# Experts of a routed mixture: a block's down product stands between the two halves of the next block's gate and up products

## The chip, the cores and the metric

The kernel runs on one core of one Trainium2 chip. The metric is the device time of one execution in microseconds. The kernel before takes 1736.07 us, the median of 3 runs (1735.58 to 1736.92).

In the text PE is TensorE, DVE is VectorE, ACT is ScalarE, POOL is GpSimd and SP is SyncE, as the profile writes them.

## The reference

One layer of a backbone over 1024 latent tokens and 256 context tokens of width 1024: modulation, one input projection into two groups of heads (a gated delta rule and a differential attention), an output projection, a layer norm, and then a mixture of experts, which is the part that the change touches. Each token chooses 2 of 32 experts, and an expert is a SwiGLU of width 512:

```
def block_ffn(args):
    xb, e = args
    return (jax.nn.silu(xb @ w_gate[e]) * (xb @ w_up[e])) @ w_down[e]
```

So a block of tokens has three products with its expert's weights: gate and up (1024 to 512 each), and then down (512 to 1024), which needs the result of the first two. All is float32. The outputs of a token's two experts are weighted and added in the last stage.

## The kernel before

The kernel is a row of stages, each of which ends with a barrier of all engines. The stage of the change is `experts`. Its work is a list of blocks of 32 token rows, sorted by expert; how many blocks there are, and which expert each has, is computed on the chip by the stage before. Four blocks are a quad (128 rows): the tokens of a quad are gathered from memory together, turned by PE (L2717, `turn_x`, at the start of each quad's body, for the next quad) and stored together by ACT (L2797).

What happens to one block b, by engine:

- PE makes the gate and up products in one go, `hidden(b, ...)` (L2725), eight steps of the contraction in two halves of four; each half waits until the weights of its last step are in `now["hidden"]`. The down product is `down(b, ...)` (L2737), four steps. It waits for the turned hidden rows of its block (`h_turned`) and for all four parts of `now["down"]` (`copied["down"]`).
- ACT takes the silu of the gate half (`gate`, L2775), after the last step of `hidden(b)`.
- DVE multiplies by the up half (L2835) and turns the result by 32x32 squares (L2839); both are `mix`. Later it scales the down product into the output tile (`keep_y`, L2831).

The weights of the current expert lie in one set of tiles, `now["hidden"]` and `now["down"]`, that PE reads. SP loads the next experts' weights from memory into `raw` tiles (L2336), three places deep for gate and up and two for down; a place is loaded again once its copy has been made. Where the expert changes between block b and block b+1, the new weights are copied over the old ones, part by part as PE has done with each:

- DVE copies the gate and up weights (`copy_hidden`, L2819, eight copies) while PE is at `hidden(b)`, ahead of `mix(b)` in DVE's program.
- ACT copies the down weights (`copy_down`, L2782, four copies) in its body for block b, each after PE has done the step of `down(b)` that reads the old ones.

All of it is written as one body for each block, and each engine runs its own body in order. ACT's body for block b is, in this order:

```
shape(i + u, 1 - u, X_PARTS[s])
gate(b + 1, (s + 1) % SUBS)
with act.If(here < after):
    copy_down(here + 1, b)
```

`shape` (L2767) writes a part of the next quad's turned tokens. `gate(b + 1)` waits for all eight steps of `hidden(b + 1)`, so the copies of `copy_down` stand behind it. PE's body works one block ahead in the same way: in the body of block b stand `hidden(b + 1)` and `down(b)`.

Of the kernel before, what the change touches and what calls it, by code (L numbers as in the profile page):

```python
# [2576 lines left out]
def experts(m):  # L2577
# [34 lines left out]
    def blocks(eng, start=None, block=None, end=None):  # L2612


        nb = eng.value_load(plan[0:1, PLAN_BLOCKS:], min_val=LOW * SUBS, max_val=BLOCKS)

        def run(part, *of):
            if part:
                part(*of)

        with ExitStack() as deeper:
            for q in range(QUADS):
                if q >= LOW:
                    deeper.enter_context(eng.If(nb > q * SUBS))
                run(start, q, q // 2, q % 2)
                with ExitStack() as inner:
                    for s in range(SUBS if block else 0):
                        if q >= LOW and s:
                            inner.enter_context(eng.If(nb > q * SUBS + s))
                        block(q, q // 2, q % 2, s)  # L2630
                run(end, q, q // 2, q % 2)
        return nb

    def place_of(eng, b):

        return eng.value_load(ranks[0:1, b:b + 1], min_val=0, max_val=NE - 1)
# [18 lines left out]
    def by_blocks(ap):  # L2655
        return ap.rearrange("p (w b x) -> p w b x", w=2, x=SUB)

    def columns_of(ap, j):

        return ap.rearrange("p w (b j x) -> p j w b x", j=SUBS, x=SUB)[:, j]  # L2660

    def hidden_bank(s):
        return m.bank(2 + s % 2, 2 * P)

    def down_bank(s):
        return m.bank(5 + s % 2, WIDE)

    with nc.Block() as block:
        @block.sync
        def _(sp):  # L2670
            experts_ = sp.value_load(plan[0:1, PLAN_EXPERTS:PLAN_EXPERTS + 1], min_val=2, max_val=NE)
            nq = sp.value_load(plan[0:1, PLAN_QUADS:PLAN_QUADS + 1], min_val=LOW, max_val=QUADS)
            def follow(place, u):

                for part in expert_loader(m, sp, place, u, copied if u > 1 else None):
                    part()

            AHEAD = 2 * SLOTS
            follow(1, 1)
            with sp.If(2 < experts_):  # L2680
                follow(2, 2)
            with sp.Fori(0, (NE - 3 + AHEAD - 1) // AHEAD) as i:
                for u in range(3, 3 + AHEAD):
                    with sp.If(AHEAD * i + u < experts_):
                        follow(AHEAD * i + u, u)

            sp.wait_ge(copied["hidden"], experts_ * KD)
            for t in range(TL):
                sp.dma_start(x1[t][:, :], d["x1"][t]).then_inc(early, 16)
            sp.dma_start(rep_ln[:, :, :], d["rep_ln"].rearrange("p (w n) -> p w n", w=4)[:, 2:4, :]).then_inc(early, 16)  # L2690

            sp.wait_ge(nothing_ready, 1)
            with sp.Fori(0, QUADS - LOW) as j:
                with sp.If(nq < j + LOW + 1):
                    sp.dma_start(flat(one(ybq, j + LOW)).rearrange("p (k n) -> p k n", k=KD), nothing[:, :].unsqueeze(1).to_broadcast([P, KD, D // KD])).then_inc(nothing_stored, 16)
                with sp.If(j + LOW < nq):
                    sp.sem_inc(nothing_stored, 16)
            sp.wait_ge(nothing_stored, 16 * (QUADS - LOW))
            sp.sem_inc(all_stored, 1)
# [11 lines left out]
        @block.tensor  # L2711
        def _(pe):
            def turn_x(i, u):
                pe.wait_ge(gathered[u], 16 * i + 16)
                pe.wait_ge(x_kept[1 - u], i + u)
                for k in range(KD):
                    last = nc.tensor.transpose(m.bank(k // 4)[:, k % 4 * P:(k % 4 + 1) * P], xg[u][:, k * P:(k + 1) * P], ident)  # L2717
                last.then_inc(x_turned[u], 1)

            def hidden(b, u, s, place, ks):  # L2720

                pe.wait_ge(copied["hidden"], place * KD + ks[-1] + 1)
                for k in ks:
                    for j in range(SUBS):
                        last = nc.tensor.matmul(by_blocks(hidden_bank(s)[j * SUB:(j + 1) * SUB, :]), xm[u][:, k, s * SUB:(s + 1) * SUB],  # L2725
                                                columns_of(now["hidden"][:, :, k, :], j), start=(k == 0), stop=(k == KD - 1),
                                                tile_position=(0, j * SUB))
                    last.then_inc(used["hidden"], 1)

            def down(b, s, place):  # L2730
                pe.wait_ge(h_turned, b + 1)
                if b >= 1:
                    pe.wait_ge(y_kept, b - 1)
                pe.wait_ge(copied["down"], place * KE + KE)
                for k in range(KE):
                    for j in range(SUBS):
                        last = nc.tensor.matmul(down_bank(s)[j * SUB:(j + 1) * SUB, :], hT[s % 2][:, k * SUB:(k + 1) * SUB],  # L2737
                                                now["down"][:, k, j * WIDE:(j + 1) * WIDE], start=(k == 0), stop=(k == KE - 1),
                                                tile_position=(0, j * SUB))
                    last.then_inc(used["down"], 1)  # L2740

            def body(q, i, u, s):
                b = q * SUBS + s
                here, after = place_of(pe, b), place_of(pe, b + 1)
                v, r = (u, s + 1) if s + 1 < SUBS else (1 - u, 0)
                if r == 0:
                    pe.wait_ge(x_kept[v], i + u + 1)
                pe.wait_ge(mixed, b)
                hidden(b + 1, v, r, after, range(KD // 2))
                hidden(b + 1, v, r, after, range(KD // 2, KD))  # L2750
                down(b, s, here)

            turn_x(0, 0)
            pe.wait_ge(x_kept[0], 1)
            first = place_of(pe, 0)
            hidden(0, 0, 0, first, range(KD // 2))
            hidden(0, 0, 0, first, range(KD // 2, KD))
            blocks(pe, lambda q, i, u: turn_x(i + u, 1 - u), body)

        @block.scalar  # L2760
# [310 lines left out]
```

## Time and profile before

| | |
|---|---|
| median of 3 runs | 1736.07 us |
| the profiled execution | 1734.94 us |
| its span | 1733.1 us |
| PE busy | 1517.3 us, 88% of the span |
| DVE busy | 927.7 us, 54% |
| ACT busy | 692.2 us, 40% |
| first `hidden` in a block's body | 1204.73 us |
| last `down` | starts at 1667.91 us |
| gate and up matmuls (L2725) | 4992, of 293.7 us in all |
| down matmuls (L2737) | 2464, of 147.4 us in all |
| blocks with a down product | 77 |
| changes of expert | 21 |

One execution was profiled, and its times run from the start of the span. Every matmul of the program stands twice in the trace: one block has 32 for gate and up in the program and 64 rows in the trace, and 16 and 32 for down. The 77 blocks follow from 2464 rows by 32, the 21 changes from the 84 copies of L2782 by four. Matmuls overlap, so busy time is not a sum of their durations. A row of the timeline gives the start, the time that it covers, engine, line, operation and tiles, and how many instructions it merges; in brackets stands the idle time of the engine ahead of it and what ended that.

### The profile page before, as it was taken

The numbers are of one execution on the slowest core, as the hardware profiler recorded it, in microseconds if no ns is written. First come the engines' busy times: TensorE is split into PE (matmuls) and PEld (weight loads), VectorE is DVE, ScalarE is ACT, GpSimd is POOL, SyncE is SP. The second block draws the span as 40 slices with busy tenths as digits, with TensorE's granted clock in tenths as the row PEclk, the third lists the DMA queues.
The fourth block names the chain that finished last, engine by engine and source line by source line (L and its number), as shares of the span: only waits on it lengthen the run. The fifth ranks groups of instructions, "written<-read, shape, count | busy, mean of one in ns | idle before, by whom it ended". The sixth has DMA issues, their size and how long they took to land. (4 is left out here: it accounts for less than half of the span.)

```text
span 1733.1 us, 47260 instructions
## 1 busy us (share of the span) xinstructions
PE 1517.3 (88%) x19436; PEld 1107.4 (64%) x19436; DVE 927.7 (54%) x1862; ACT 692.2 (40%) x1585; POOL 191.5 (11%) x266
## 2 busy tenths in 40 slices
PE   5799998999968899979998888954999999998768
PEld 3588885779857788856666567743555555554333
DVE  6798752341124565658999846774142454343416
ACT  5544431012234545536667734422141433433321
POOL 0000100000043544400000000000000000000015
PEclk9899998999978999989999998966999999999989
DMA  9312315450133344230020044318849789999976
GB/s 360 122 61 80 128 46 203 172 176 26 61 121 108 114 124 118 85 138 19 13 74 19 7 144 158 122 52 324 309 174 346 290 322 397 398 397 393 358 233 256
DMA packets 154396, 305.33 MB, mean 176 GB/s; under 512 B 10718, under 2 KB 57390, under 8 KB 150834
## 3 DMA queue, kind: packets, MB, share of 16 engines
q1 hardware_dynamic: 132306, 244.94, 39.1%
q0 software_dynamic: 10336, 46.67, 7.6%
q10 hardware_dynamic: 11520, 10.49, 1.9%
q8 instruction: 161, 2.64, 0.6%
q14 instruction: 73, 0.60, 0.1%
HBM read 256.40 MB, written 45.66 MB: 174 GB/s over the span
## 5 line engine op out<-in xcount | busy, mean ns | idle before, releaser
L2725 PE MATMUL psum<-now_hidden,i_xm 128*32 128x256 f32 x4992 | 293.7, 388 | 23.7 <-DVE now_hidden L2819 17.2
L2725 PEld LDWEIGHTS psum<-now_hidden,i_xm 128*32 128x32 f32 x4992 | 160.1, 112 | 149.4 <-issue 32.6
L2737 PE MATMUL psum<-now_down,i_hT 128*32 128x256 f32 x2464 | 147.4, 379 | 5.8 <-ACT now_down L2782 5.8
L2835 DVE TENSOR_TENSOR i_h<-i_silu,psum 128x128 f32<-128x128 f32 x78 | 22.3, 286 | 215.7 <-ACT i_silu L2775 215.7
L2767 ACT ACTIVATE i_xm<-psum,modT 128x128 f32<-128x128 f32 x163 | 63.3, 457 | 161.7 <-issue 130.0
L2819 DVE COPY now_hidden<-raw_hidden 128x1024 f32 x168 | 104.1, 694 | 36.5 <-DMA raw_hidden<-in_w_up 27.9
L2737 PEld LDWEIGHTS psum<-now_down,i_hT 128*32 128x32 f32 x2464 | 81.0, 110 | 59.2 <-ACT now_down L2782 9.1
L1911 PE MATMUL psum<-dkT,f_qT 64*128 64x512 f32 (+1 forms) x384 | 90.4, 577 | 23.7 <-ACT f_E L1962 21.2
L123 PE MATMUL psum<-hT_head,wm_head 128*128 128x512 f32 (+1 forms) x256 | 97.6, 381 | 10.7 <-DVE hT_rest L414 6.4
L1962 ACT ACTIVATE f_E<-psum,f_mx 128x1280 f32<-128x1280 f32 (+2 forms) x96 | 92.1, 967 | 15.8 <-DVE f_mx L2021 15.7
L123 PE MATMUL psum<-hT_head,wm_rest 128*128 128x512 f32 (+1 forms) x256 | 96.0, 375 | 0.0
L123 PE MATMUL psum<-hT_rest,wm_head 128*128 128x512 f32 (+1 forms) x256 | 95.7, 374 | 0.0
L2782 ACT ACTIVATE now_down<-raw_down 128x1024 f32 x84 | 81.9, 1054 | 12.9 <-DMA raw_down<-in_w_down 8.5
L2775 ACT ACTIVATE i_silu<-psum 128x128 f32<-128x128 f32 x78 | 21.7, 278 | 162.9 <-PE psum L2725 162.2
L1931 PE MATMUL psum<-dv,f_AT 128*128 128x128 f32 x640 | 85.3, 279 | 0.8 <-ACT f_AT L1968 0.6
L1931 PEld LDWEIGHTS psum<-dv,f_AT 128*128 128x128 f32 x640 | 78.4, 194 | 6.5 <-issue 3.0
L123 PE MATMUL psum<-wt_rest,hT_head 128*128 128x512 f32 x208 | 82.2, 395 | 0.0
L1968 ACT ACTIVATE f_AT<-psum 128x512 f32<-128x512 f32 (+1 forms) x96 | 50.5, 526 | 71.7 <-PE psum L1921 71.7
L1494 ACT ACTIVATE e_pc<-psum 128x128 f32<-128x128 f32 x100 | 26.5, 284 | 126.0 <-PE psum L1354 124.9
L661 DVE SCALAR_TENSOR_TENSOR conv<-padded,cw,conv 128x1282 f32<-128x1282 f32 x48 | 74.6, 1555 | 1.7
L2282 PE MATMUL psum<-w_out_head,g_yT 128*128 128x512 f32 x128 | 56.2, 439 | 14.8 <-ACT g_yT L1794 10.4
L2020 DVE TENSOR_REDUCE f_mx<-psum 128x1 f32<-128x768 f32 x64 | 60.8, 951 | 15.0 <-PE psum L1911 15.0
(377 smaller groups left out, 2986.5 us busy)
## 6 DMA issues: line engine op xcount, KB each, us to landing
raw_hidden<-in_w_gate SPq DMA_DIRECT2D x22, 2048.0 KB, 19.9
raw_hidden<-in_w_up SPq DMA_DIRECT2D x22, 2048.0 KB, 24.9
raw_down<-in_w_down SPq DMA_DIRECT2D x22, 2048.0 KB
wa_late<-in_w_ada POOLq DMA_DIRECT2D x16, 1024.0 KB, 5.5
yb<-i_y ACTq DMA_DIRECT2D x80, 128.0 KB, 7.4
wa<-in_w_ada SPq DMA_DIRECT2D x8, 1024.0 KB, 13.2
wt<-in_w_in SPq DMA_DIRECT2D x4, 2048.0 KB, 7.8
wm<-in_w_in SPq DMA_DIRECT2D x12, 512.0 KB, 3.7
```

The source lines that it names most:

```text
L123: last = nc.tensor.matmul(out, a, b, start=(first and n == 0), stop=(final and n == 2))
L661: ins = nc.vector.scalar_tensor_tensor(y, padded[u][:, j:j + wide], cw[:, c * CONV + j:c * CONV + j + 1], y, ALU.mult, ALU.add)
L1911: last = nc.tensor.matmul(scores(c, key, key + w), qT[t % 2][rows, h, :], dkT[rows, h, key:key + w], start=True, stop=True)
L1931: last = nc.tensor.matmul(m.bank(7, P, h * P), AT[n % 2][:, t, :], dv[:, t, h * P:(h + 1) * P], start=(t == 0), stop=(t == TT - 1))
L1962: nc.scalar.activation(E[n % 2][c][:, a:z], scores(c, a, z), ACT.Exp, bias=mx[n % 2][c][:, 2:3], scale=SC, accum_out=rs[n % 2][c][:, part: ...
L2020: link(nc.vector.tensor_reduce(x[:, 1:2], scores(c, NC, TOK), AX, ALU.max))
L2282: nc.tensor.matmul(m.bank(2 + c), yT[t % 2][:, k, :], w[:, k, here], start=(k == 0 and n == 0), stop=False)
L2725: last = nc.tensor.matmul(by_blocks(hidden_bank(s)[j * SUB:(j + 1) * SUB, :]), xm[u][:, k, s * SUB:(s + 1) * SUB], columns_of(now["hidden" ...
L2737: last = nc.tensor.matmul(down_bank(s)[j * SUB:(j + 1) * SUB, :], hT[s % 2][:, k * SUB:(k + 1) * SUB], now["down"][:, k, j * WIDE:(j + 1) ...
L2767: last = nc.scalar.activation(xm[u][:, k, :], m.bank(k // 4)[:, k % 4 * P:(k % 4 + 1) * P], ACT.Identity, scale=modT[:, 4 * KD + k, 0:1], ...
L2782: nc.scalar.activation(now["down"][:, k, :], down_slot(place, k), ACT.Copy).then_inc(copied["down"], 1)
L2819: nc.vector.tensor_copy(now["hidden"][:, :, k, :], loaded[:, :, k, :]).then_inc(copied["hidden"], 1)
```

## The change

In PE's body for a block, `down(b)` moves ahead of the second half of `hidden(b + 1)`. Nothing else changes: the same instructions, with the same waits, on every engine.

```diff
                 pe.wait_ge(mixed, b)
                 hidden(b + 1, v, r, after, range(KD // 2))
+                down(b, s, here)
                 hidden(b + 1, v, r, after, range(KD // 2, KD))
-                down(b, s, here)
```

On PE, the body of the first block and the start of the second stood in this order before (L2722 is the wait of a half of `hidden`, L2734 that of `down`, L2636 loads the blocks' places in the list of experts):

```order
L2636 TENSOR_LOAD ranks
L2636 ISA x2
L2722 ISA
L2725 MATMUL psum<-now_hidden,i_xm_15268 32x256 x16
L2722 REGISTER_ALU
L2725 MATMUL psum<-now_hidden,i_xm_15268 32x256 x16
L2734 ISA
L2737 MATMUL psum<-now_down,i_hT_15265 32x256 x16
L2636 TENSOR_LOAD ranks
L2636 ISA x2
```

The same place of PE's program in the changed kernel:

```order
L2636 TENSOR_LOAD ranks
L2636 ISA x2
L2722 ISA
L2725 MATMUL psum<-now_hidden,i_xm_15268 32x256 x16
L2734 ISA
L2737 MATMUL psum<-now_down,i_hT_15265 32x256 x16
L2722 REGISTER_ALU
L2725 MATMUL psum<-now_hidden,i_xm_15268 32x256 x16
L2636 TENSOR_LOAD ranks
L2636 ISA x2
```

The 16 down matmuls and their wait now stand behind 16 of the 32 gate and up matmuls instead of behind all of them; the other 16 end the body.

On ACT nothing moves. A body with the silu (L2775), the branch on a change of expert (L2790) and the four copies (L2782), in both kernels:

```order
L2767 ACTIVATE i_xm_15269<-psum,modT 128x128 x3
L2775 ACTIVATE i_silu<-psum 128x128
L2790 COMPARE_AND_BRANCH
L2644 ISA
L2645 ISA
L2782 REGISTER_ALU
L2782 ISA
L2782 ACTIVATE now_down<-raw_down 128x1024
L2782 ISA
L2782 ACTIVATE now_down<-raw_down 128x1024
```

What moves is the event for which the silu waits: the last gate and up matmul now stands behind the down product of its body.

## Rows read from the trace of the kernel before

**Rows 1.** The page: the span, and the group of the down weight copies

```profile
span 1733.1 us, 47260 instructions
...
L2782 ACT ACTIVATE now_down<-raw_down 128x1024 f32 x84 | 81.9, 1054 | 12.9 <-DMA raw_down<-in_w_down 8.5
```

**Rows 2.** Windows: busy us (count) of PE, PEld, DVE, ACT, POOL, then PEclk, DMA share, GB/s

```profile
1240.00:1280.00 40.00, 39.64 (x696) 23.51 (x692) 17.54 (x39) 8.16 (x21) 1.87 (x2) 1.00 0.32 99
1425.00:1640.00 215.00, 198.49 (x3368) 113.96 (x3357) 86.72 (x190) 80.89 (x150) 8.60 (x9) 0.98 1.04 396
```

**Rows 3.** Who waited for whom, 1198 to 1672: us in total, times, longest

```profile
PE psum L2725 <- DVE now_hidden L2819: 17.2, 5, 7.1
...
PE psum L2737 <- ACT now_down L2782: 5.8, 7, 1.9
```

**Rows 4.** Timeline, one block, no change of expert: PE and the silu

```profile
1301.95 3.66 PE L2725 MATMUL psum<-now_hidden,i_xm 128*32 128x256 f32 x64
...
1305.43 1.91 PE L2737 MATMUL psum<-now_down,i_hT 128*32 128x256 f32 x32
...
1305.68 0.28 ACT L2775 ACTIVATE i_silu<-psum 128x128 f32<-128x128 f32 x1 [2.93 <-PE psum L2725]
...
1307.31 3.66 PE L2725 MATMUL psum<-now_hidden,i_xm 128*32 128x256 f32 x64
```

**Rows 5.** Timeline, the expert changes in two blocks in a row

```profile
1348.62 4.91 DVE L2819 COPY now_hidden<-raw_hidden 128x1024 f32 x8 [0.19 <-PE psum L2725]
...
1350.37 1.92 PE L2737 MATMUL psum<-now_down,i_hT 128*32 128x256 f32 x32
...
1351.27 3.90 ACT L2782 ACTIVATE now_down<-raw_down 128x1024 f32 x4 [0.37 <-PE psum L2737]
...
1353.76 0.31 DVE L2839 STREAM_TRANSPOSE i_hT<-i_h 128x128 f32<-128x128 f32 x1
...
1355.69 1.92 PE L2737 MATMUL psum<-now_down,i_hT 128*32 128x256 f32 x32
```

**Rows 6.** Timeline, copies right behind their silu, and the down product behind them

```profile
1277.66 0.28 ACT L2775 ACTIVATE i_silu<-psum 128x128 f32<-128x128 f32 x1
1277.82 3.91 ACT L2782 ACTIVATE now_down<-raw_down 128x1024 f32 x4
...
1281.78 1.93 PE L2737 MATMUL psum<-now_down,i_hT 128*32 128x256 f32 x32 [0.46 <-ACT now_down L2782]
```

**Rows 7.** Timeline, quad ends: transposes once, the first and last copies there

```profile
1363.02 1.09 PE L2717 MATMUL psum<-mask,i_x 128*128 128x128 f32 x8
...
1364.65 1.06 ACT L2782 ACTIVATE now_down<-raw_down 128x1024 f32 x1 [2.94 <-DMA raw_down<-in_w_down]
...
1630.85 2.00 ACT L2782 ACTIVATE now_down<-raw_down 128x1024 f32 x2 [0.34 <-PE psum L2737]
```

**Rows 8.** Timeline of PE: first hidden of a body, last down product

```profile
1204.73 3.66 PE L2725 MATMUL psum<-now_hidden,i_xm 128*32 128x256 f32 x64
...
1667.91 1.91 PE L2737 MATMUL psum<-now_down,i_hT 128*32 128x256 f32 x32
```

**Rows 9.** Timeline of PE: four matmul groups behind an idle time

```profile
1432.21 1.93 PE L2737 MATMUL psum<-now_down,i_hT 128*32 128x256 f32 x32 [1.94 <-ACT now_down L2782]
...
1571.42 6.45 PE L2725 MATMUL psum<-now_hidden,i_xm 128*32 128x256 f32 x64 [6.26 <-DVE now_hidden L2819]
...
1606.71 5.37 PE L2725 MATMUL psum<-now_hidden,i_xm 128*32 128x256 f32 x64 [3.11 <-DVE now_hidden L2819]
...
1645.32 5.35 PE L2725 MATMUL psum<-now_hidden,i_xm 128*32 128x256 f32 x64 [7.13 <-DVE now_hidden L2819]
```

**Rows 10.** Window of PE: length, busy us (count), granted clock, DMA share, GB/s

```profile
1609.00:1612.00 3.00, 3.00 (x40) 0.62 1.04 389
```

**Rows 11.** Timeline: a load issue behind a copy, the last expert's copies

```profile
1419.29 0.37 SPq L2336 DMA_DIRECT2D raw_down<-in_w_down  x1
...
1642.77 4.91 DVE L2819 COPY now_hidden<-raw_hidden 128x1024 f32 x8 [10.42 <-DMA raw_hidden<-in_w_up]
```

## The prediction

> **What bounds the kernel now.** First the page: the span is 1733.1 us, and the group of the down weight copies has 84 instructions, so 21 changes of expert [rows 1]. Then the windows of the experts' stage: PE is busy 39.64 of 40 us where DMA moves 99 GB/s, and 198.49 of 215 us where DMA moves 396 GB/s with all its engines busy [rows 2]. The stage is bound by PE first, and later by PE and the loads together. What PE waits for is in the waits: 17.2 us for gate and up weights and 5.8 us for down weights [rows 3]. A block without a change of expert shows a PE that waits for nothing: the gate and up matmuls start at 1301.95, the down product 3.48 us later, the next block's 1.88 us after that [rows 4]. So there is nothing for the change to win in such a block; it can only keep it. With 64 and 32 equal matmuls, a half of `hidden` and a down product are about 1.74 us each, and some 0.1 us lies between bodies.
>
> The first `hidden` of a body starts at 1204.73 and the last down product at 1667.91 [rows 8]: 463.2 us.
>
> **The change in a block without a change of expert: nothing.** The silu starts 0.07 us behind the last gate and up matmul (1301.95 + 3.66 against 1305.68), and takes 0.28 us [rows 4]; the multiplication and the turn took 0.54 us more behind the copies in [rows 5]. So `down(b)` can start some 1.0 us behind the end of `hidden(b)`. Its cover shrinks from a whole `hidden(b + 1)` (3.5 us) to a half (1.74 us), which is enough. Above nothing, a bound is 0.1 us in each of 77 blocks, should the second half be issued later for the turn between products (the gap that lies between bodies); I take nothing, since matmuls of `hidden` and down follow each other without a gap already. Below nothing: PE has no idle time there, so no gain.
>
> **The change where the expert changes: a new wait.** The copies of the down weights stand on ACT behind `gate(b + 1)`, and this now waits for a half of `hidden` that stands behind `down(b)`. Before, the silu came while `down(b)` ran, the copies went from 1351.27 to 1355.17 under the next `hidden`, and the next down product started at 1355.69, 0.5 us after them [rows 5]. Now the copies cannot begin before the second half ends. Where copies stood right behind their silu, they started 0.16 us after it, took 3.91 us, and the down product came 0.05 us behind [rows 6]. That makes 0.07 + 0.16 + 3.91 + 0.05 = 4.2 us from the last gate and up matmul to `down(b + 1)`. In that time PE has 1.7 us of work: the last matmul's own end (-0.2), the step to the next body (0.1 to 0.2), and one half of `hidden`. So PE stands still for **2.5 us** at each change. At a quad's end the eight transposes of `turn_x` add 1.0 us of cover [rows 7], and 1.5 us are left. Five of the 21 changes are there, with copies from 1364.65 to 1630.85 [rows 7]: 16 x 2.5 + 5 x 1.5 = **47.5 us**. What is queued behind the waiting down product is the second half of `hidden(b + 2)`, and behind that the next silu and the next copies, so that changes in a row (1277.82, or both in rows 5) each pay in full.
>
> **DVE is late too, a little.** It copies the gate and up weights ahead of `mix(c)`, for c the last block of an expert. Eight copies took 4.91 us, 0.61 each, and the turned rows were ready 0.54 us after them [rows 5]. Now the fifth copy waits for the first step of the second half: 3.5 us after the body's start and 0.9 us more (the lag that the first down copy shows, 1351.27 against 1350.37 in [rows 5]), and four copies and the mix end at 4.4 + 2.5 + 0.5 = 7.4 us. `down(c)` would start at 7.1. That is **0.3 us**, once for each row of changes in a row; there are ten, and in two of them the transposes lie between, so 8 x 0.3 = 2.4 us. In the others that follow, it shifts both sides.
>
> **What goes.** The old waits lie under the new ones or are served by the delay: 17.2 + 5.8 us [rows 3]. The matmuls behind the three long waits took 6.45, 5.37 and 5.35 us instead of 3.66 [rows 4, 9], at a lower clock and behind copies in progress: 6.2 us more. Together 29.2 us. PE's way through the stage is then 463.2 - 29.2 + 47.5 + 2.4 = 483.9 us, **20.7 us longer**.
>
> **The clock.** Behind an idle time of 1.94 us the next group took its usual 1.93 us; behind 3.11 us one took 5.37 instead of 3.66 [rows 9], and the granted clock of a window in it is 0.62, so part of it ran at the lower level, 1.2 of 2.4 GHz [rows 10]. The new idle times are 2.3 us (2.5 less the last matmul's end), between these two; the short ones of 1.3 us are below both. Bounds: none of 16 lowers the clock (0), or each costs 5.37 - 3.66 = 1.7 us (27 us). I take half of them, since 2.3 is in the middle third: **13.6 us**. The 32 matmuls behind the 1.94 us were no slower, so I take no more.
>
> The Trainium skill (TensorE: Matmul & The Clock Gate, section "Why this matters for your kernels") holds that throughput drops in mid-kernel are avoided as long as the idle gaps between bursts of matmuls stay below about 3 us. The trace agrees at 1.94 and at 3.11 us and has nothing between; by that rule the clock's term would be 0 and the time that of the first rival.
>
> **The loads.** The last expert's copies start at 1642.77, when their data lands, and the third restart of the loads, at 1419.29, was set by a copy's end [rows 11]. PE, without its waits so far, would now come to the last copies at about 1645.3 - 7.1 = 1638.2 [rows 9], less 20.4 (the 29.2 without this last wait and its slow matmuls), plus 47 and 12, which is 1677; the data, delayed by the stalls ahead of 1419 (below) and by later buffers, lands between 1658 and 1678. So it is mostly hidden; 1.5 us for what isn't.
>
> **Sum:** 20.7 + 13.6 + 1.5 = 35.8 us on the profiled execution's 1734.94: **1771 us**. The median of the runs is 1.1 us above that execution, which is within what I can tell.
>
> **Rivals.**
> - *The clock stays at its upper level.* For it the quiet 1.94 us, against it the 3.11 [rows 9]. 1734.9 + 20.7 + 1.5 = 1757 us.
> - *The loads bound the second part and take the stalls in.* For it 396 GB/s from 1425 on [rows 2]. Then only what stands ahead of 1419 counts: five stalls of 2.5, one of 1.5 and 0.3, less about 2.3 of the old waits, and the restart comes 1.3 us later in its body (5.6 instead of 4.4 us after its start): 13.3, and one stall behind the last load, 2.5. 1751 us. Against it: 14 more changes with 31 us, more than the 27 us that PE loses there now (29.2 less 2.3).
> - *Each stall lowers the clock.* 20.7 + 27 + 1.5: 1784 us.
> - *Faster.* The one place is the down product behind a change. Were its copies done within the 1.7 us of cover, the 5.8 us of waits for them and the 0.7 us of copies' pace inside a `hidden` would go: 1728 us. It decides whether four copies can end 1.7 us behind the last matmul; the rows say 4.2 [rows 6], and ACT's program puts them behind the silu. Little speaks for it.
> - *Nothing.* The trace would have to hide 47 us behind loads that land no later. Hardly.
>
> **Chances.** 1771: 0.50. Clock unaffected, 1757: 0.25. Loads take it in, 1751: 0.11. Clock lowered each time, 1784: 0.08. Nothing: 0.03. Faster: 0.03. The range for 8 in 10 goes from 1750 to 1783. A measurement of this kernel tells about 0.2% (3.5 us) from no change; by it faster is 0.03, the same 0.03, slower 0.94.
>
> **What would show it.** In the waits of the changed kernel, PE's down product (L2737) waits for `now_down` (L2782) about 20 times, 40 to 48 us in all, longest near 2.5 if the data is there, and the wait for L2819 shrinks. Each L2782 group starts 0.2 us behind its silu, never 0.4 us behind a down product. Blocks without a change keep their 5.4 us (1301.95 to 1307.31). SP's restarts come later, first by about 1 us at the first change. The granted clock shows dips after about half of the stalls. I am wrong if the copies run under `hidden` as before, if blocks without a change lengthen, or if PE's waits for loads at 1571, 1606 and 1645 stay as long as they were.

## The result: 1786.5 us, 3.0% slower, and the profile after

The changed kernel takes 1786.51 us, the median of 4 runs (1782.27 to 1789.36), and the kernel before 1735.82 in 4 runs (1733.81 to 1736.92): a ratio of 1.030 (95% interval 1.028 to 1.032). The forecast was slower, 1771 us in a range of 1750 to 1783. The direction and the place hold; the size is 15 us too small, and outside the range. The profiled execution takes 1785.22 us, with a span of 1783.4, 50.3 more than before.

The page of the changed kernel has the group of the copies of [rows 1], and the two groups of matmuls. Behind the second bar stand the idle time ahead of a group, and what ended most of it:

```profile
span 1783.4 us, 47260 instructions
...
L2725 PE MATMUL psum<-now_hidden,i_xm 128*32 128x256 f32 x4992 | 309.7, 390 | 6.9 <-DVE now_hidden L2856 3.9
...
L2737 PE MATMUL psum<-now_down,i_hT 128*32 128x256 f32 x2464 | 162.3, 406 | 53.5 <-ACT now_down L2782 52.2
...
L2782 ACT ACTIVATE now_down<-raw_down 128x1024 f32 x84 | 81.8, 1045 | 6.2 <-issue 6.0
```

PE stood 53.5 us ahead of down products, and 52.2 of them ended with a copy of down weights by ACT. The waits of the same stretch as in [rows 3], to 1725 since the stage ends later:

```profile
PE psum L2737 <- ACT now_down L2782: 52.2, 21, 3.0
...
PE psum L2737 <- DVE i_hT L2839: 1.2, 5, 0.3
...
PE psum L2725 <- DVE now_hidden L2819: 0.7, 3, 0.3
```

The wait for `now_down` is there in all 21 changes of expert, and is 52.2 us where it was 5.8. The wait for gate and up weights (L2819), 17.2 us before, is 0.7. The place of [rows 5] and its neighbours in the timeline, where the expert changes three times in a row:

```profile
1362.14 1.93 PE L2737 MATMUL psum<-now_down,i_hT 128*32 128x256 f32 x32 [0.26 <-DVE i_hT L2839]
...
1363.89 3.77 PE L2725 MATMUL psum<-now_hidden,i_xm 128*32 128x256 f32 x64
...
1365.87 0.28 ACT L2775 ACTIVATE i_silu<-psum 128x128 f32<-128x128 f32 x1 [3.39 <-PE psum L2725]
1366.42 3.90 ACT L2782 ACTIVATE now_down<-raw_down 128x1024 f32 x4 [0.27 <-issue]
...
1370.37 1.93 PE L2737 MATMUL psum<-now_down,i_hT 128*32 128x256 f32 x32 [2.71 <-ACT now_down L2782]
...
1378.60 3.15 PE L2737 MATMUL psum<-now_down,i_hT 128*32 128x256 f32 x32 [2.58 <-ACT now_down L2782]
...
1388.51 1.93 PE L2737 MATMUL psum<-now_down,i_hT 128*32 128x256 f32 x32 [1.67 <-ACT now_down L2782]
```

The second half of `hidden` runs behind the down product (1363.89; the timeline merges it with the next half), the silu starts behind that (1365.87), the copies start 0.55 us after the silu's start and end at 1370.32, and the down product follows 0.05 us later. The next one starts 8.23 us after it and takes 3.15 us instead of 1.93; 9.91 us lie from it to the third, 1.7 more than 8.23. A block without a change, as in [rows 4]:

```profile
1206.12 1.91 PE L2737 MATMUL psum<-now_down,i_hT 128*32 128x256 f32 x32
...
1209.82 0.28 ACT L2775 ACTIVATE i_silu<-psum 128x128 f32<-128x128 f32 x1 [3.29 <-PE psum L2725]
...
1211.47 1.92 PE L2737 MATMUL psum<-now_down,i_hT 128*32 128x256 f32 x32
```

From down product to down product it takes 5.35 us, and took 5.36 before (1301.95 to 1307.31 in [rows 4], for the matmuls ahead). There the change costs nothing. The granted clock, in windows of the whole stage and of one slow down product (PE busy with its count, PEclk, DMA share, GB/s), as in [rows 2] and [rows 10]:

```profile
1206.00:1717.00 511.00, 454.57 (x7460) 0.96 0.83 306
1293.10:1296.10 3.00, 3.00 (x36) 0.62 1.03 387
```

The slow down product at 1293.10 (2.99 us) ran in part at the lower clock, 1.2 GHz. Of the 21 down products behind such a wait 13 took 2.67 to 3.41 us, and 8 took 1.93. The loads set hardly anything any more: the last expert's copies, which waited for their data in [rows 11], wait for PE:

```profile
1692.72 2.50 DVE L2819 COPY now_hidden<-raw_hidden 128x1024 f32 x4 [1.36 <-PE psum L2725]
```

and SP's own queue waits for ACT's copies more than before (252.9 us in 16 waits, before 139.1 us in 10), so the loads have slack:

```profile
SPq L2336 <- ACT now_down L2782: 252.9, 16, 53.8
```

Where the 50.3 us are is seen by adding up PE's time from the first down product (1208.21 before, 1206.12 after) to the last (1667.91 and 1716.79), 76 steps in each kernel. The idle times are the gaps between matmul rows, by the group that follows them; the low clock's part is an estimate, half of PE's busy time in the stretches in which the granted clock is down. The other kernels below are in the table too, each from one profile.

| kernel | first to last down | idle ahead of down | idle ahead of gate and up | low clock | rest |
|---|---|---|---|---|---|
| before | 459.7 | 5.8 | 19.8 | 6.3 | 427.9 |
| changed | 510.7 | 53.5 | 2.9 | 22.2 | 432.1 |
| e1_filled | 511.4 | 15.4 | 13.6 | 0 | 482.3 |
| e9_filled_narrow | 525.3 | 17.0 | 10.8 | 18.3 | 479.2 |
| e5_filled_one | 509.4 | 45.9 | 4.9 | 16.9 | 441.7 |
| e8_branch_first | 495.9 | 45.7 | 3.7 | 15.1 | 431.4 |
| e2_six_of_eight | 472.9 | 28.9 | 10.0 | 3.4 | 430.6 |
| e6_copies_first_after | 467.2 | 22.9 | 4.2 | 6.3 | 433.8 |
| e7_copies_first_before | 461.2 | 8.9 | 19.6 | 3.3 | 429.5 |
| e3_tiny_copies_after | 457.5 | 5.8 | 15.5 | 6.4 | 429.8 |
| e4_tiny_copies_before | 453.1 | 0 | 20.6 | 6.2 | 426.3 |
| e10_shared_before | 461.0 | 0 | 27.1 | 7.1 | 426.9 |
| e11_shared_copies_first | 463.5 | 23.7 | 6.6 | 1.6 | 431.6 |

So 51.0 us more lie in this stretch: 47.7 of idle time ahead of down products, 15.9 of low clock, 4.2 in the rest (each of 21 waits also lays bare some 0.2 us of a matmul's end), less 16.9 of old idle time ahead of gate and up. From the stage's end to the span's end little moved (63.3 us before, 63.0 after).

### The profile page after: what moved, and what is told of

Its sections match the earlier page's. It is cut to its first block and busy times, and to the rows that moved or that the text cites. A ratio compares the mean times of both kernels' runs of the same rounds, so it can differ in the third digit from the quotient of the medians.

```text
span 1783.4 us, 47260 instructions
## 1 busy us (share of the span) xinstructions
PE 1533.5 (86%) x19436; PEld 1109.6 (62%) x19436; DVE 923.8 (52%) x1862; ACT 694.6 (39%) x1585; POOL 190.8 (11%) x266
## 5 line engine op out<-in xcount | busy, mean ns | idle before, releaser
L2725 PE MATMUL psum<-now_hidden,i_xm 128*32 128x256 f32 x4992 | 309.7, 390 | 6.9 <-DVE now_hidden L2856 3.9
L2725 PEld LDWEIGHTS psum<-now_hidden,i_xm 128*32 128x32 f32 x4992 | 164.8, 113 | 135.3 <-issue 38.3
L2737 PE MATMUL psum<-now_down,i_hT 128*32 128x256 f32 x2464 | 162.3, 406 | 53.5 <-ACT now_down L2782 52.2
L2775 ACT ACTIVATE i_silu<-psum 128x128 f32<-128x128 f32 x78 | 21.7, 278 | 247.9 <-PE psum L2725 247.8
L2819 DVE COPY now_hidden<-raw_hidden 128x1024 f32 x168 | 105.1, 691 | 20.4 <-PE psum L2725 17.4
L2782 ACT ACTIVATE now_down<-raw_down 128x1024 f32 x84 | 81.8, 1045 | 6.2 <-issue 6.0
L2705 POOL DMA_INDIRECT i_x<-xn,tok x20 | 19.4, 972 | 476.4 <-PE psum L2717 476.4
```

What stands on the lines that cost most here:

```text
L2782: nc.scalar.activation(now["down"][:, k, :], down_slot(place, k), ACT.Copy).then_inc(copied["down"], 1)
L2819: nc.vector.tensor_copy(now["hidden"][:, :, k, :], loaded[:, :, k, :]).then_inc(copied["hidden"], 1)
```

## The experiments

The forecast's chain has three parts that can be taken apart: the copies that stand behind the silu, the silu that stands behind the second half, and the clock after the wait. Theory A is the forecast's mechanism with its prices; the rivals (B, C) are named in each expectation. Each ratio is to the kernel before as it was timed beside that kernel; its medians lie between 1734.61 and 1737.61 us, so a median can be compared with another kernel's to about 3 us.

### Without the copies' length: e3_tiny_copies_after, e4_tiny_copies_before

The same edit in the changed kernel and in the kernel before:

```diff
-nc.scalar.activation(now["down"][:, k, :], down_slot(place, k), ACT.Copy)
+nc.scalar.activation(now["down"][:, k, 0:8], down_slot(place, k)[:, 0:8], ACT.Copy)
```

> The changed kernel whose four down weight copies at a change of expert copy 8 of 1024 columns each (the rest of the new expert's down weights is left out). Theory A (the copies behind the silu are the whole path): no wait of PE for now_down above 0.5 us, no dip of the clock, and a time within 4 us of the kernel before with the same small copies, near 1730 us. Theory B (the order itself costs): 8 us or more above that one.

> The kernel before with the same small copies (the rest of the new expert's down weights is left out). Both theories: the waits for now_down (5.8 us) go, the down places come free earlier, and the loads then bound: 1724 to 1734 us. It is the base for the changed kernel with small copies.

Measured: 1735.95 us (ratio 0.999, 0.997 to 1.000) and 1728.01 us (0.994, 0.992 to 0.996). The waits of the changed order with tiny copies:

```profile
PE psum L2725 <- DVE now_hidden L2819: 13.8, 5, 6.0
...
PE psum L2737 <- DVE i_hT L2839: 5.7, 14, 1.1
```

and of the order before with them:

```profile
PE psum L2725 <- DVE now_hidden L2819: 18.6, 5, 7.1
```

The wait for `now_down` is gone from both: with the copies shortened, some 43 of the 51 us of the change are gone. So most of the cost is the copies' length behind the silu, and not the order of matmuls as such. Yet the two differ by 8 us in their medians (the interval of neither reaches the other) and by 4.4 in the stretch of the table (457.5 and 453.1), where A wanted at most 4 between them and B 8 or more: A holds for 43 of the 51 us, and the order has a cost of its own. What the trace has for it is PE's wait for the turned hidden rows, 5.7 us in 14 places, which the other order does not have: DVE, whose last four copies now stand behind the second half, is late. The remaining 3 to 4 us lie behind the stage (66.0 and 62.5 us from its end to the span's), with a longer low clock there; one profile of each can't say whether that belongs to the edit.

### Copies ahead of the silu: e6_copies_first_after, e7_copies_first_before

Again one edit in both orders:

```diff
-                gate(b + 1, (s + 1) % SUBS)
                 with act.If(here < after):
                     copy_down(here + 1, b)
+                gate(b + 1, (s + 1) % SUBS)
```

> The changed kernel with ACT's copies of the down weights ahead of the silu instead of behind it. They can then start 0.9 us behind the start of the down product and lie under the second half of gate and up. Theory A: a change of expert costs PE some 0.5 us (the silu now waits for the copies) instead of 2.9, no dip of the clock behind it: 1734 to 1744 us. Theory B (the order itself costs 15 us): 1748 us or more.

> The kernel before with ACT's copies ahead of the silu. Here the copies start 0.9 us behind the down product, after the last gate and up matmul, and end 4.8 us behind it; then silu and mix take 1.0 us, against 5.4 us of cover. Both theories: 0.4 us more wait per change, partly under the loads: 1736 to 1746 us. It tells whether the order on ACT alone does anything.

Measured: 1740.80 us (1.004, 1.002 to 1.006) and 1736.94 us (1.001, 0.999 to 1.003). The timeline of e6 at two changes in a row:

```profile
1281.21 3.89 ACT L2782 ACTIVATE now_down<-raw_down 128x1024 f32 x4
1285.00 0.27 ACT L2775 ACTIVATE i_silu<-psum 128x128 f32<-128x128 f32 x1
...
1286.08 3.60 PE L2737 MATMUL psum<-now_down,i_hT 128*32 128x256 f32 x32 [3.37 <-DVE i_hT L2839]
...
1290.29 2.50 DVE L2819 COPY now_hidden<-raw_hidden 128x1024 f32 x4 [1.36 <-PE psum L2725]
...
1292.79 0.29 DVE L2835 TENSOR_TENSOR i_h<-i_silu,psum 128x128 f32<-128x128 f32 x1
...
1293.56 1.94 PE L2737 MATMUL psum<-now_down,i_hT 128*32 128x256 f32 x32 [0.29 <-DVE i_hT L2839]
```

The copies now run under the second half (1281.21 to 1285.10), and it is the silu that comes late: behind it stand the multiplication and the turn, and the down product starts 1.08 us after the silu, with 3.37 us of waiting on DVE's rows in this one. In a row of changes, DVE then takes over: its last four copies end at 1292.79, the multiplication and the turn follow, and the down product starts at 1293.56. The step from one down product to the next has a median of 6.4 us over the 21 blocks with a change, against 8.2 in the changed kernel, and is 5.78 where DVE's copies set it. This one edit takes 46 of the 51 us away. It is the clearest answer: the change costs what it does because ACT's copies are chained behind a silu that it made late. e7 shows what ACT's new order costs by itself: a step with a change has a median of 6.3 us there (6.1 in the kernel before), with 8.5 us of waits for the turned rows. The two are 4 us apart, about what the table leaves between e3 and e4. It is not a gain, though: neither version beats the kernel before. Of the 22.9 us of idle time ahead of e6's down products, 14 lie in four waits of 3.37 to 3.60 us, each at a quad's start, where ACT has just issued the stores of the quad before and comes late (the copies at 1281.21 start 4.1 us behind their block's down product, those of the next block 1.4).

### The branch and the waits ahead of the silu: e8_branch_first

The trace of the changed kernel has 0.55 us between the starts of silu and copies, where the forecast used 0.16. Here the branch and the waits for the loads stand ahead of the silu:

```diff
-                gate(b + 1, (s + 1) % SUBS)
                 with act.If(here < after):
+                    wait_down_loaded(act, here + 1)
+                    gate(b + 1, (s + 1) % SUBS)
                     copy_down(here + 1, b)
+                with act.If(after < here + 1):
+                    gate(b + 1, (s + 1) % SUBS)
```

with the wait for the loads taken out of `copy_down`.

> The changed kernel with ACT's branch on a change of expert, and the waits for the loads, ahead of the silu instead of between silu and copies. In the changed kernel the copies start 0.55 us behind the silu's start, where my sum had 0.16. Theory A (that gap is ACT's own branch and register work behind a wait): the gap falls to 0.2 to 0.35 us, each wait of PE by as much, and with fewer dips of the clock the time is 1770 to 1781 us. Theory B (the gap is a delay between silu and copy of its own): the gap stays and the time is 1784 to 1790 us.

Measured: 1774.05 us (1.023, 1.020 to 1.026). The timeline:

```profile
1284.84 0.28 ACT L2775 ACTIVATE i_silu<-psum 128x128 f32<-128x128 f32 x1 [2.78 <-issue]
1285.04 3.90 ACT L2781 ACTIVATE now_down<-raw_down 128x1024 f32 x4
...
1288.99 1.93 PE L2737 MATMUL psum<-now_down,i_hT 128*32 128x256 f32 x32 [2.34 <-ACT now_down L2781]
...
1296.90 3.31 PE L2737 MATMUL psum<-now_down,i_hT 128*32 128x256 f32 x32 [2.24 <-ACT now_down L2781]
```

The copies start 0.20 us after the silu, as [rows 6] had it, and a step with a change takes 7.92 us instead of 8.23; gap and time are as A had them. Idle time ahead of down falls by 7.8 us and the low clock by 7.1, with 9 low stretches instead of 13. With about the gap that the forecast had assumed, the kernel takes nearly what the forecast said: 12.5 us of the miss of 15 go with this gap, by the table half of them directly and half by way of the clock. How many waits lower the clock is read from one profile of each kernel, so the second half is less sure.

### The down product behind six of eight steps: e2_six_of_eight

```diff
-                hidden(b + 1, v, r, after, range(KD // 2))
+                hidden(b + 1, v, r, after, range(6))
                 down(b, s, here)
-                hidden(b + 1, v, r, after, range(KD // 2, KD))
+                hidden(b + 1, v, r, after, range(6, KD))
```

> The down product stands behind six of the eight steps instead of four. Theory A: the cover grows by 0.87 us, each wait shrinks by that (21 x 0.87 = 18 us), the idle times of 1.7 us no longer lower the clock (about 20 us more), and loads take part of it: 1746 to 1754 us, no dip of the clock behind a wait for the down weights. Theory B: only the 18 us go, 1766 to 1770 us.

Measured: 1752.36 us (1.009, 1.007 to 1.011). The waits:

```profile
PE psum L2737 <- ACT now_down L2782: 28.9, 21, 2.1
...
PE psum L2725 <- DVE now_hidden L2819: 7.2, 7, 2.8
```

The wait falls from 52.2 to 28.9 us, 1.1 for each change; two steps more are 0.87 us more cover (half of 1.74), and the step with a change, 7.37 us in the median, is shorter than the 8.23 of the changed kernel by as much. The clock gives more back: 3.4 us of it are left. Behind the waits of up to 1.98 us no down product is slow; the two slow ones stand behind 2.00 and 2.07 us. A expected no slow one at all. PE meets more of the old waits again (7.2 us for L2819, 0.7 in the changed kernel), as it comes to the weights earlier.

### PE busy through the wait: e1_filled, e5_filled_one, e9_filled_narrow

Ahead of the down product behind a change, PE multiplies the identity by itself into a bank that nothing reads, eight times in e1, once in e5. In e9 it does so eight times with 8 columns instead of 128, so that its program is as long as e1's:

```diff
                 hidden(b + 1, v, r, after, range(KD // 2))
+                if b >= 1:
+                    with pe.If(place_of(pe, b - 1) < here):
+                        for _ in range(8):
+                            nc.tensor.matmul(m.bank(7, P), ident, ident, start=True, stop=True)
                 down(b, s, here)
```

> The changed kernel with eight 128x128 matmuls of the identity into an unused PSUM bank ahead of the down product of each block whose expert differs from that of the block before; they lie in the time in which PE waits for the down weights (2.5 to 2.8 us idle in 16 of 21 cases). Theory A (idle times of that length lower the clock, 13 periods of 3.4 us at the lower level cost some 20 us): PE's idle time before L2737 falls to 1 us or less each, the granted clock stays at its upper level in the stage, and the time is 1764 to 1770 us. Theory B (the low clock costs little, and the 15 us beyond my sum come from the order itself: more issue time, later copies on DVE): 1783 to 1788 us.

> The control of e1: the same branch on PE in each block, with one filling matmul instead of eight, so that PE still stands idle for over 2 us at most changes of expert and the clock falls again. e1 had no dip of the clock in the stage and still took 1789.8 us, with 12.8 us of idle time that its rows put to issue (2 us in the changed kernel). Theory A: the branch costs what the clock gave back; with the branch and the low clock together the time is 1804 to 1812 us. Theory B (the low clock costs little): within 4 us of e1, 1786 to 1794 us.

> A closer control of e1 than e5 was: the same branch and the same eight filling matmuls, each with 8 columns instead of 128, so that PE's program is as long as in e1 and yet PE is idle for about 2 us at a change. In e1's trace the low clock is gone (22 us in the changed kernel), but 18 us turn up as idle time ahead of gate and up matmuls (13.6 us) and in blocks without a change. Theory A (those 18 us come with the longer program in the branch, and the low clock costs what the rows say): 1800 to 1810 us, with both. Theory B (the low clock costs nothing that filling gives back, the idle times only move): 1784 to 1792 us, like e5.

Measured: 1789.83 us (1.030, 1.028 to 1.033), 1786.82 (1.031, 1.027 to 1.034) and 1800.77 (1.039, 1.036 to 1.041). A had expected a gain from e1, and it isn't there. The timeline of e1 at a change shows that the mechanism works, though:

```profile
1301.54 2.05 PE L2753 MATMUL psum<-mask 128*128 128x128 f32 x16
...
1304.20 1.93 PE L2737 MATMUL psum<-now_down,i_hT 128*32 128x256 f32 x32 [0.61 <-ACT now_down L2786]
```

The identity matmuls take 2.05 us of the wait, and the down product takes its 1.93 us. There is no low stretch in the whole stage, and the granted clock is 1.00. But the page of e1 has another idle time:

```profile
L2725 PE MATMUL psum<-now_hidden,i_xm 128*32 128x256 f32 x4992 | 306.5, 382 | 17.6 <-issue 8.9
```

PE now stands 17.6 us ahead of gate and up, 8.9 of them waiting for nothing that the profile shows. The table accounts for it: against the changed kernel, 22.2 us of low clock are gone, and there are 10.7 more idle ahead of gate and up, 4.9 more of filling (43.0) and idle (15.4) together than the old 53.5, and 7.2 more in the rest. So what came with the filling, 22.8 us, costs as much as the clock gave back. It is not the branch as such, which PE passes in every block: e5 has the same branch over one matmul, and by the table it costs little.

```profile
L2725 PE MATMUL psum<-now_hidden,i_xm 128*32 128x256 f32 x4992 | 309.2, 391 | 8.9 <-DVE now_hidden L2860 3.9
```

Idle time ahead of gate and up is 4.9 us in e5 (2.9 in the changed kernel), the rest less its filling (10.3) is 431.4 (432.1), and filling and idle ahead of down are 56.2 together (53.5): 4.0 us in all, where e1 has 22.8 and e9, with eight narrow matmuls, 18.5. So the cost comes with the eight matmuls behind the branch, and why eight that are mostly passed over cost this much no run shows. A's 1804 to 1812 for e5 took the branch alone for the cause and was wrong; that e5 is within 3 us of e1 fits B, but with 16.9 us of low clock and a cheaper program it fits the account above as well.

e9 is the control with an equal program. The timeline of e9, one change:

```profile
1304.01 1.95 PE L2753 MATMUL psum<-mask 128*128 128x8 f32 x16
...
1306.62 3.32 PE L2737 MATMUL psum<-now_down,i_hT 128*32 128x256 f32 x32 [0.66 <-ACT now_down L2786]
```

The narrow matmuls hold PE for 1.95 us, nearly as long as the wide ones, and the down product behind them takes 3.32 us. e9 has 11 low stretches, 18.3 us of low clock against e1's 0, and is 10.9 us longer in the median (12.8 with each taken against the kernel before beside it) and 13.9 in the stretch. That is in A's 1800 to 1810, and B's "nothing" is out. The experiment puts 11 to 14 us on 11 low stretches, 1.0 to 1.3 us each, where the rows put 1.7; outside the low clock, e1 has 4.3 us more than e9 in the table's other columns, which hides that much. e1's miss lies in the means, not in the mechanism.

### Half of the copies on POOL: e10_shared_before, e11_shared_copies_first

If the copies' length is what counts, sharing it out may beat both kernels. POOL takes copies 2 and 3 in a block body of its own, and ACT keeps 0 and 1. e10 is that in the kernel before, e11 in e6:

```diff
+            def share(q, i, u, s):
+                b = q * SUBS + s
+                here, after = place_of(pool, b), place_of(pool, b + 1)
+                with pool.If(here < after):
+                    wait_down_loaded(pool, here + 1)
+                    for k in range(2, KE):
+                        pool.wait_ge(used["down"], b * KE + k + 1)
+                        nc.gpsimd.tensor_copy(now["down"][:, k, :], down_slot(here + 1, k)).then_inc(copied["down"], 1)
```

> The kernel before with the last two of the four down weight copies on POOL, which is idle. The copies then end some 2 us earlier, the waits of 5.8 us go in part, and the loads restart 2 us earlier. The kernel with small copies took 9.6 us less than before. Theory A (copies and the restart of the loads behind them are what is left to gain): 1728 to 1734 us, with before at 1735. Rival (POOL's copies are slow or slow DVE's): 1738 us or more.

> The changed kernel with ACT's copies ahead of the silu and two of the four on POOL. The copies end before the second half of gate and up does, so the silu no longer waits for them (in e6 PE waited 21.7 us for the turned rows). Theory A: what is left is 0.46 us for DVE's copies in 8 of the changes, against loads that restart 3 to 4 us earlier: 1728 to 1736 us, no dip of the clock behind a down product. Rival (POOL's copies are slow or slow DVE's): 1740 us or more.

Measured: 1738.51 us (1.002, 1.001 to 1.003) and 1740.82 (1.004, 1.002 to 1.006). Neither is a gain, as the rivals had it. The group of POOL's copies in e10 (shortest, median and longest in ns, then first and last start), and that of DVE's:

```profile
L2716 POOL COPY now_down<-raw_down x42: 1027/1042/2027, 1281.9 to 1658.2; 128x1024 f32 x42
```

```profile
L2828 DVE COPY now_hidden<-raw_hidden x168: 674/686/1526, 1271.2 to 1652.3; 128x1024 f32 x168
```

A copy on POOL takes as long as one on ACT (1042 ns in the median), but DVE's copies beside it get as long as 1526 ns, where the longest was 912 in the kernel before. Their median stays at 686: 11 of the 168 are longer than 950 ns, and each of the 11 runs beside a copy on POOL, as in this group, which took 4.91 us in [rows 5]:

```profile
1283.42 7.30 DVE L2828 COPY now_hidden<-raw_hidden 128x1024 f32 x8 [0.18 <-issue]
...
1287.24 2.94 POOL L2716 COPY now_down<-raw_down 128x1024 f32 x2 [2.96 <-PE psum L2746]
```

The 5.8 us of waits for down weights did go (0 in the table), and came back ahead of gate and up, 27.1 us instead of 19.8. So the gain went into slower copies of the gate and up weights. That POOL's copies slow DVE's was seen in length and place alone; no run moved POOL's copies away from DVE's.

No version ran faster than the kernel before, except the two that leave most of the copies out (e4 by 0.6%, e3 by 0.1%).

## Why the forecast had the right mechanism and too small a size

By the forecast's own sum the stretch from first to last down product would have been 459.7 - 29.2 + 49.9 + 13.6 + 1.5 = 495.5 us; it is 510.7.

- **"The change in a block without a change of expert: nothing."** Right: 5.35 us a block, before and after.
- **"So PE stands still for 2.5 us at each change."** The place, the chain and the 21 times are right, and so is the shorter stall at a quad's end. The size is not. The step that failed is *"Where copies stood right behind their silu, they started 0.16 us after it"*. In [rows 6] the silu itself has no waiting time ahead of it: ACT was late there. Where ACT waits for PE's last matmul, the branch, the waits and the register work that stand between silu and copies in its program take their time after the silu, and the copies start 0.55 us after it, 0.4 us later, in 16 of the 21 changes (0.84 in three). The changed kernel has the short gap too, in the first of its changes, where the silu had no wait:

```profile
1279.07 0.28 ACT L2775 ACTIVATE i_silu<-psum 128x128 f32<-128x128 f32 x1
1279.23 3.90 ACT L2782 ACTIVATE now_down<-raw_down 128x1024 f32 x4
```

Worked out again by the rows of the timeline, 1.75 (down product, 1362.14 to 1363.89) + 1.98 (second half and start of the silu, to 1365.87) + 0.55 + 3.90 + 0.05 is the step of 8.23 us, 2.9 more than a block without a change takes. That is 21 x 0.4 = 8.4 us. e8 takes it away and gets 7.8 us of idle time back, and 7.1 more from the clock.
- **"That is 0.3 us, once for each row of changes in a row."** DVE's lateness was right in kind and measures 0.46 us in those 8 blocks, 3.7 us instead of 2.4 (5.78 us for a step that DVE sets, less 5.3 for one without a change). e3 against e4 shows it alone: PE waits 5.7 us for the turned rows, and the order costs 4.4 to 8 us even with no copies to wait for. With the term before this one, stalls come to 57.7 us (53.5 idle and 4.2 of matmul ends) where the forecast had 49.9.
- **"I take half of them" (the clock).** This is the other term that was too small, and by a like amount. The price of one, 1.7 us, was right by the rows (9.91 - 8.23), and e9 against e1 gives 1.0 to 1.3 by experiment. The count was not: 13 of 21 instead of 8, 22.2 us of low clock instead of 13.6. Part of that may follow from the first error, since the waits are longer than reckoned; e8, with shorter waits, has 9 low stretches. That half of them would do it was a choice between two rows, not a reading. The Trainium skill (TensorE: Matmul & The Clock Gate, section "Why this matters for your kernels") puts the bound at gaps of about 3 us, and by it none of these waits would have lowered the clock; the measurement decides against it, since all 13 slow down products stand behind waits of 1.97 to 2.98 us, 12 of them of 2.80 or less.
- **"What goes."** Right: the waits for gate and up weights fell from 17.2 to 0.7 us, and the old ones for down weights lie under the new ones.
- **"The loads": 1.5 us.** Nothing was left of it. Copies at 1692.72 wait for PE. The rival by which the loads take the stalls in is out.
- **The terms together.** Stalls 7.8 us too small, the clock 8.6 too small, the loads 1.5 too large: 14.9 of the 15.2 us between 510.7 and 495.5.
- **The rivals.** The clock at its upper level (1757) is out by the rows and by e9. "Each stall lowers the clock", at 1784 and with a chance of 0.08, was nearest to the time, but by luck: it needs all 16 of the longer waits to lower the clock, 12 of them and one of the shorter ones did, and the rest of its size came from ACT's 0.4 us.

What stays open: why 8 of the waits left the clock alone. The four of 1.67 us all did, but so did waits of 2.71, 2.71, 2.85 and 2.98 us, where others of 2.71 and 2.98 did not. The length of a wait alone doesn't decide it: e6 has three waits of 3.37 to 3.60 us with the low clock behind them, and this one of 3.59 without.

```profile
1526.92 1.93 PE L2737 MATMUL psum<-now_down,i_hT 128*32 128x256 f32 x32 [3.59 <-DVE i_hT L2839]
```

In the changed kernel the granted clock fell 0.3 to 1.0 us after the start of the down product behind the wait, never at once; so the moment at which a wait falls may count as well as its length. No run moved a wait to see. How the 3 to 4 us behind the stage in e3 against e4 come about is open too.

## What to carry to other kernels

Moving a product ahead of another's second half makes all that waits for the second half late, on every engine: before such a move, follow what stands in program order *behind* the operation that becomes late (here four copies behind a silu), for it is that chain that PE pays for. The price of a chain has to be read at a place where the engine waits as it will then wait: a gap read behind an instruction that was itself late leaves out the branch and register work that the lateness hid. And where PE is to stand still for 2 to 3 us many times over, as here, the lower clock belongs in the sum for more than half of those times (13 of the 17 waits of that length, and 9 of 16 in e8).

## What the runs showed of the hardware that was not expected

- An idle time of PE of 1.97 to 2.98 us was followed by a down product at the lower clock (2.67 to 3.41 us instead of 1.93) 13 times in the changed kernel, and at 1.2 GHz in part (granted clock 0.62 in the window). But for e9's, no wait of up to 1.94 us did this (nine of 1.58 to 1.84 us in e2, five of 1.94 in e11).
- Matmuls of 8 columns filled 1.95 us of PE's wait, and the clock still fell behind them 11 times (e9); matmuls of 128 columns filled 2.05 us, and it never did (e1). The kernel with the narrow ones is 11 to 14 us longer.
- Between a silu that had waited and the copies behind a branch lay 0.55 us from start to start; with the branch and the waits ahead of the silu it was 0.20 us (e8).
- With a branch over eight matmuls in PE's program, idle time ahead of gate and up was 13.6 us in the stage instead of 2.9, 8.9 us of all such waits behind nothing that the profile shows (e1); with the same branch over one matmul it was 4.9 (e5).
- A copy of 128x1024 float32 on POOL took 1042 ns in the median and 2027 at most, and the longest of DVE's copies went from 912 to 1526 ns (e10), all 11 of its long ones beside a copy on POOL.
